# First expert visited: its turned rows by products with a one-hot matrix, its number changed to 1, and the shares behind its up product

## The reference, cut to what matters

```
h = rmsnorm(x) * g_ffn
g = argmax(h @ w_r1 + b_r1)                      # one of 4 groups, by token
e = top 2 of (h @ w_r2 + b_r2)[group g]          # two of its 4 experts
share = group probability * normalised expert probability
hid = silu(h @ w_gate[e]) * (h @ w_up[e])        # 1024 -> 256
out = x + sum over the two e of share * (hid @ w_down[e])   # 256 -> 1024
```

## Time and profile before

| | us |
|---|---|
| median of 3 runs | 1452.06 |
| the profiled execution, its own time | 1451.33 |
| its span in the trace | 1449.4 |
| last r_hot ready (DVE L2709) | 1221.9 |
| first transpose of expert rows (PE L1470) | 1234.9 |
| first up product starts (PE L1477) | 1237.8 |
| second up product starts | 1250.4 |
| last product of an expert ends (PE) | about 1431 |

### The profile page before, as it was taken

How to read it: one execution, slowest core, us unless ns; L and a number is a source line. 1 busy time by engine, 2 the same in 40 slices (tenths; PEclk the granted TensorE clock), 3 DMA queues, 4 the chain that set the end, 5 groups by cost and what they waited for, 6 DMA issues and landing times.

```text
span 1449.4 us, 16277 instructions
## 1 busy us (share of the span) xinstructions
PE 1326.3 (92%) x6144; PEld 982.7 (68%) x6144; DVE 563.8 (39%) x1294; ACT 539.9 (37%) x952; POOL 408.4 (28%) x203
## 2 busy tenths in 40 slices
PE   3999989889899999999998999999899996899996
PEld 3788666457678766765877777888787785444443
DVE  2164353534320135236897453234423315121225
ACT  4353434343542447445333554323433333111111
POOL 3255221014555222233423112543115322000002
PEclk9999999979999999999999999999999997899999
DMA  4232434013444221221322112432034605989915
GB/s 146 65 102 75 158 103 132 17 52 124 139 126 160 73 58 59 59 73 46 114 66 94 45 45 66 163 106 73 8 147 129 250 27 205 384 318 371 331 59 190
DMA packets 76474, 179.60 MB, mean 124 GB/s; under 512 B 11217, under 2 KB 22791, under 8 KB 69735
## 3 DMA queue, kind: packets, MB, share of 16 engines
q1 hardware_dynamic: 68656, 165.48, 33.7%
q0 software_dynamic: 2624, 8.41, 1.6%
q10 hardware_dynamic: 5110, 4.62, 1.1%
HBM read 153.32 MB, written 25.17 MB: 123 GB/s over the span
## 4 chain that ended last, share of the span: by engine, by line
PE 43%; DVE 8%; ACT 2%; issue 1%; DMA 1%; POOL 0%; DVEq 0%; ACTq 0%
PE ps L993 8%; PE ps L1477 8%; PE ps L995 8%; PE ps L994 8%; PE ps L1484 4%; DVE work L2551 1%; PE ps L1371 1%; PE ps L1354 1%; DVE dq L2560 1%; DVE best L2549 1%; PE ps L1470 1%; PE ps L1327 1%; DVE mix_lo L2330 1%; PE ps L1399 1%; PE ps L1361 1%
## 5 line engine op out<-in xcount | busy, mean ns | idle before, releaser
L877 POOL TENSOR_TENSOR w_lo<-raw,w_hi 128x1024 fp32r<-128x1024 f32 (+1 forms) x158 | 377.7, 2407 | 786.2 <-ACT w_hi L1691 786.2
L993 PE MATMUL ps<-w_hi,act_hi 128*128 128x512 f32 (+1 forms) x560 | 234.7, 419 | 6.9 <-POOL w_lo L877 3.6
L1691 ACT ACTIVATE w_hi<-raw 128x1024 fp32r<-128x1024 f32 (+1 forms) x158 | 158.9, 1033 | 169.3 <-PE ps L995 160.7
L994 PE MATMUL ps<-w_lo,act_hi 128*128 128x512 f32 (+1 forms) x560 | 220.3, 393 | 0.0
L995 PE MATMUL ps<-w_hi,act_lo 128*128 128x512 f32 (+1 forms) x560 | 219.6, 392 | 0.0
L993 PE MATMUL ps<-w_hi,mix_hi 128*128 128x512 f32 x320 | 131.8, 412 | 9.9 <-DVE mix_lo L2330 6.4
L993 PEld LDWEIGHTS ps<-w_hi,act_hi 128*128 128x128 f32 (+1 forms) x560 | 105.0, 187 | 47.2 <-issue 13.8
L995 PE MATMUL ps<-w_hi,mix_lo 128*128 128x512 f32 x320 | 126.3, 395 | 0.0
L994 PE MATMUL ps<-w_lo,mix_hi 128*128 128x512 f32 x320 | 126.2, 394 | 0.0
L995 PEld LDWEIGHTS ps<-w_hi,act_lo 128*128 128x128 f32 (+1 forms) x560 | 104.8, 187 | 25.4
L994 PEld LDWEIGHTS ps<-w_lo,act_hi 128*128 128x128 f32 (+1 forms) x560 | 105.0, 188 | 24.0 <-issue 1.5
(11 more groups left out here) (447 smaller groups left out, 1925.4 us busy)
## 6 DMA issues: line engine op xcount, KB each, us to landing
raw<-in_w_in SPq DMA_DIRECT2D x92, 512.0 KB, 3.5
gu<-in_w_gate SPq DMA_DIRECT2D x16, 1024.0 KB, 6.1
gu<-in_w_up SPq DMA_DIRECT2D x16, 1024.0 KB, 8.5
dn<-in_w_down SPq DMA_DIRECT2D x16, 1024.0 KB, 9.8
x_rows<-zeros SPq DMA_DIRECT2D x16, 512.0 KB, 4.9
raw<-in_w_out SPq DMA_DIRECT2D x16, 512.0 KB, 3.9
raw<-in_w_mem_kv SPq DMA_DIRECT2D x16, 512.0 KB, 3.7
xe<-x_rows SPq DMA_DIRECT2D x16, 512.0 KB, 9.1
```

Of the source, the lines that this page charges most:

```text
L877: pool.tensor_tensor(lo[:, 0:a], raw[:, g % RAW_SLOTS, 0:a], hi[:, 0:a].bitcast(F32), ALU.subtract).then_inc(*POOL.done(("w_lo", g)))
L993: pe.matmul(dst, l_hi, r_hi, start=start, stop=False, skip_group_check=skip)
L994: pe.matmul(dst, l_hi, r_lo, start=False, stop=False, skip_group_check=skip)
L1691: nc.scalar.activation(split_slot(g)[0][:, 0:a], raw[:, g % RAW_SLOTS, 0:a], ACTF.Copy).then_inc(*ACT.done(("w_hi", g)))
```

## The change

The expert visited first is now number 1, and number 0 the second (`expert_of`). Its rows aren't read back from DRAM. On VectorE `place` also makes a one-hot matrix for each token block, token by slot of expert 1. PE multiplies the normalised rows of each block with it (`x_hot(t)`), eight products per block, accumulated over the four blocks in banks 0 and 1; the sum is the turned rows, ready for the same two VectorE copies. The count of tokens becomes a step of its own (`counts`) behind `x_hot(3)`. The shares (`r_weights`), the overflow flag and both `last_hot` move behind the first up product, the making of `oh` (`last_oh`) being split from its use; the SiLU table is loaded at the end of ScalarE's `r_weights`. The up product waits for each half of `xeT` where it needs it. SP reads rows for visits 1, 2 and 3 at once, and issues set 5 (which lies over `xs_ffn`) behind the last `x_hot`.

```
+def expert_of(visit):
+    return (FIRST_E, 0)[visit] if visit < 2 else visit          # FIRST_E = 1

-    order += [("r_turn", 3), ("route", 1, 1), ("rank", 1), ("pos", 1), ("r_stat", 3), ("r_logits", 3), ("route", 2), ("rank", 2), ("pos", 2)]
-    order += [("r_weights",), ("last_hot", 0), ("over_flag",), ("x_turn", 0)]
+    order += [("r_turn", 3), ("x_hot", 0), ("route", 1, 1), ("rank", 1), ("pos", 1), ("r_stat", 3), ("r_logits", 3)]
+    order += [("x_hot", 1), ("x_hot", 2), ("route", 2), ("rank", 2), ("pos", 2), ("x_hot", 3), ("counts",), ("x_turn", 0)]
+    order += [("r_weights",)]
     for e in range(N_EXP):
         order += [("up", e)] + [("x_turn", e + 1)] * (e + 1 < N_EXP) + [("down", e - 1)] * (e > 0) + [("turn", e)]
-        if e == 2:
-            order += [("last_hot", 1)]
+        order += [("over_flag",)] * (e == 0) + [("last_hot", e - 1)] * (1 <= e <= 2) + [("last_oh", e)] * (e < 2)
...
             sp.wait_ge(scattered, 16 * 2 * NT)
-            for e in range(X_BUFS):
-                sp.dma_start(xe[:, e, :], expert_rows(x_rows, e)).then_inc(xe_in[e], 16)
+            for e in range(1, X_BUFS + 1):
+                sp.dma_start(xe[:, e % X_BUFS, :], expert_rows(x_rows, expert_of(e))).then_inc(xe_in[e % X_BUFS], 16)
             for e in (4, 5):
+                if e == 5:
+                    sp.wait_ge(*PE.after("xT", 0, 1))
                 load_up(sp, e, e, gu_in[e])
...
+            def x_hot(t):
+                if t == 0:
+                    for half in range(2):
+                        claim(half, (DVE, ("xeT", 0, half)))
+                pe.wait_ge(*ACT.after("xs_ffn", t))
+                pe.wait_ge(*DVE.after("hot", t))
+                for k in range(KC):
+                    mm = pe.matmul(ps[:, k // 4, P * (k % 4):P * (k % 4) + P], xs_ffn[:, t, P * k:P * k + P], oh[t // 2][:, t % 2, :],
+                                   start=(t == 0 and k % 4 == 0), stop=(t == NT - 1), skip_group_check=True)
+                    if t == NT - 1 and k % 4 == 3:
+                        mm.then_inc(*PE.done(("xT", 0, k // 4)))
...
             def up_product(bank, s, i, turned=None):
                 for k in range(KC):
+                    if turned is not None and k % 4 == 0:
+                        pe.wait_ge(*DVE.after("xeT", turned, k // 4))
                     mm = pe.matmul(ps[:, bank, :], xeT[:, i, k, :], gu[s][:, :, k, :], start=(k == 0), stop=(k == KC - 1))
...
                 act.wait_ge(*DVE.after("r_d"))
                 nc.scalar.activation(rt[:, 9, 0:4], rt[:, 9, 0:4], ACTF.Exp).then_inc(*ACT.done(("r_ed",)))
+                tables(SILU)
...
                 link(dve.tensor_tensor(r_at[:, a:b, :], r_hot[:, a:b, :], r_at[:, a:b, :], ALU.mult))
+                dve.wait_ge(*DVE.after("first_slots"))
+                for t in ts:
+                    dve.tensor_scalar(oh[t // 2][:, t % 2, :], first_slots[:, :], r_at[:, t, FIRST_E:FIRST_E + 1], None,
+                                      ALU.is_equal).then_inc(*DVE.done(("hot", t)))
...
-            def last_hot(i):
+            def last_oh(i):
...
                 hot.then_inc(*DVE.done(("oh", i)))
+
+            def last_hot(i):
+
                 dve.wait_ge(*PE.after("slot_share", i))
```

More of the change, by code:

```diff
@@ L158 @@
 E_SETS = 6
+FIRST_E = 1
 LAST_E = (N_EXP - 2, N_EXP - 1)
@@ L514, in program @@
         slots = sb("slots", [P, P], 129.75)
+        first_slots = sb("first_slots", [P, P], 130.25)
         tl = sb("tl", [P, 24], 133.75)
@@ L784, in first_sets @@
                         sp.wait_ge(*PE.after("m_O", NT * MEM_H - 1))
-                        load_up(sp, 0, 0, gu_in[0])
+                        load_up(sp, expert_of(0), 0, gu_in[0])
                     elif u == 1:
-                        load_down(sp, 0, 0, dn_in[0])
+                        load_down(sp, expert_of(0), 0, dn_in[0])
                 elif name == "w_out20":
@@ L790, in first_sets @@
                         sp.wait_ge(*PE.after("unit", first_unit["gate21"] + KC // 2 - 1))
-                        load_up(sp, 1, 1, gu_in[1])
+                        load_up(sp, expert_of(1), 1, gu_in[1])
                     elif u == 1:
-                        load_down(sp, 1, 1, dn_in[1])
+                        load_down(sp, expert_of(1), 1, dn_in[1])
                 elif name == "w_out21":
@@ L842, in _ @@
                     load_up(sp, e + E_SETS, e % E_SETS, gu_in[e % E_SETS])
-                if e + X_BUFS < N_EXP:
+                if 0 < e and e + X_BUFS < N_EXP:
                     sp.wait_ge(*PE.after("xT", e, 1))
@@ L854, in _ @@
                 sp.wait_ge(*DVE.after("ye", e - 1))
-                sp.dma_start(expert_rows(y_rows, e - 1), ye[:, (e - 1) % 2, :]).then_inc(ye_out[(e - 1) % 2], 16)
+                sp.dma_start(expert_rows(y_rows, expert_of(e - 1)), ye[:, (e - 1) % 2, :]).then_inc(ye_out[(e - 1) % 2], 16)
             for t in range(NT):
@@ L1456, in rank_rows, with counts @@
                 mm.then_inc(*PE.done(("ranked", i)))
[L1457 to L1462, removed]
+            def counts():
+                claim(6, (DVE, ("over",)))
+                for t in range(NT):
+                    mm = pe.matmul(ps[:, 6, 80:96], all_ones[:, :], r_hot[:, t, :], start=(t == 0), stop=(t == NT - 1),
+                                   skip_group_check=True)
+                mm.then_inc(*PE.done(("counts",)))
+            def x_hot(t):
[9 more added lines that the diff above has]
+                        mm.then_inc(*PE.done(("xT", 0, k // 4)))
             def x_turn(e):
+                if e == 0:
+                    return
                 for half in range(2):
                     claim(half, (DVE, ("xeT", e, half)))
-                pe.wait_ge(xe_in[e % X_BUFS], 16 * (e // X_BUFS + 1))
+                pe.wait_ge(xe_in[e % X_BUFS], 16 * ((e - 1) // X_BUFS + 1))
                 for k in range(KC):
@@ L1472, in x_turn, with up_product @@
                         tr.then_inc(*PE.done(("xT", e, k // 4)))
-            def up_product(bank, s, i):
+            def up_product(bank, s, i, turned=None):
                 for k in range(KC):
+                    if turned is not None and k % 4 == 0:
+                        pe.wait_ge(*DVE.after("xeT", turned, k // 4))
                     mm = pe.matmul(ps[:, bank, :], xeT[:, i, k, :], gu[s][:, :, k, :], start=(k == 0), stop=(k == KC - 1))
@@ L1497, in up @@
                 claim(2 + e % 2, (ACT, ("e_silu", e)), (DVE, ("hid", e)))
-                for half in range(2):
-                    pe.wait_ge(*DVE.after("xeT", e, half))
-                up_product(2 + e % 2, e % E_SETS, e % 2).then_inc(*PE.done(("up", e)))
+                up_product(2 + e % 2, e % E_SETS, e % 2, e).then_inc(*PE.done(("up", e)))
             def turn(e):
@@ L1658, in _ @@
                     rank_rows(*a)
+                elif step == "counts":
+                    counts()
+                elif step == "x_hot":
+                    x_hot(*a)
                 elif step == "x_turn":
@@ L2655, in r_start @@
                 dve.wait_ge(route_in, 16 * 8)
+                dve.tensor_scalar(first_slots[:, :], slots[:, :], float(FIRST_E), None, ALU.add).then_inc(*DVE.done(("first_slots",)))
                 dve.tensor_tensor(w_rg[:, :, :], w_r[:, :, :], gains[:, GAINS["g_ffn_2"]:GAINS["g_ffn_2"] + KC].unsqueeze(2).to_broadcast([P, KC, 20]),
@@ L3027, in _ @@
                      "mem_values": mem_values, "r_stat": r_stat, "r_logits": r_logits, "route": route, "pos": place, "r_weights": r_weights,
-                     "x_turn": x_turn, "up": up, "down": down, "last_hot": last_hot, "add": add, "last_rows": last_rows}
+                     "x_turn": x_turn, "up": up, "down": down, "last_oh": last_oh, "last_hot": last_hot, "add": add, "last_rows": last_rows}
             for step, *a in order:
```

## The result

| | before | changed |
|---|---|---|
| median, first set of runs | 1452.06 us (5) | 1439.07 us (5) |
| ratio, 95% interval | | 0.9898 [0.9872, 0.9924] |
| ratio of a second set (e1) | | 0.9893 [0.9874, 0.9913] |
| profiled execution, its own time / span | 1451.33 / 1449.4 us | 1434.36 / 1432.4 us |

The forecast was 1438.8 us, with 1435.3 to 1443.5 as the range. The two profiled executions differ by 17.0 us, more than the medians do. Part of that isn't the change's: the first `rank`, which stands ahead of nearly all of it, comes at 1197.02 here and came at 1199.38 before.

The account below looks back on a forecast made before the run. PE, busy 92% of the span, was taken as the bound, with time to gain in the seam before the experts and the second last_hot. Terms -12.3 - 1.3 + 0.3 = -13.3 us gave 1438.8 us, range 1435.3 to 1443.5.

Parts of the forecast that it names:

- part 1: Seam between routing and experts: one-hot products replace scatter wait, read and transposes; up(0) starts at 1228.2 against 1237.75.
- part 2: First up product: the clock comes back earlier within it, so it takes 8.0 us, before 9.05.
- part 3: From up(0)'s end to up(1): no table load (-1.28) and a half wait (-0.55) leave 1.8 to 1.9 of 3.6 us.
- part 4: Both last_hot on PE's path, oh made long before, no clock fall: -1.3 us (bounds -1.8 and +1.7).
- part 5: Expert visits: the second wait inside each up product costs 0.3 us in all (bounds 0 and 2.2); tail unchanged.
- Rival B: Expert visits: transfers catch up with PE, some 0.5 us wait each over six, giving 1441.8 us; chance 0.10.
- Rival A: Seam between routing and experts: the clock stays low throughout, giving 1445.3 us; chance 0.10.

Follow-up runs that it names:

- e1: The changed kernel run again with no edit: 1436.29 us median, ratio 0.9893 to the kernel before.
- e3: Changed kernel with all four blocks of one-hot products behind the last pos instead of in PE's gaps: 1445.25 us, ratio 0.9946 to the kernel before.
- e2: Changed kernel with the new order alone, no one-hot products, first visit's rows read back and transposed: 1447.57 us, ratio 0.9974 to the kernel before.
- e4: Changed kernel with the SiLU table loaded in front of the first SiLU again; one trace: up(1) 10.34 us behind up(0) instead of 9.06.
- e5: Changed kernel with both xeT halves awaited in front of the up product; one trace: up(1) 9.49 us behind up(0) instead of 9.06.
- e6: Changed kernel plus five idle products behind x_hot(2) and five behind the last rank; one trace: up(0) 28.0 us behind the first rank.
- e8: Changed kernel with counts before x_hot(3), last_hot(0) behind up(0), five idle products behind x_hot(2): 1438.81 us, ratio 0.9873 to the kernel before.
- e9: Changed kernel plus a 1 MB DRAM copy behind each refill of experts 6 to 13; one trace, 3.6 us longer than e1's from the rank.
- e12: Changed kernel with counts before x_hot(3) and last_hot(0) between up(0) and the second visit's transposes: 1435.49 us, ratio 0.9882 to the kernel before.
- e10: Changed kernel plus five idle products between the last rank and x_hot(3); one trace: up(0) 27.1 us behind the first rank.

## Why the prediction was right, by its steps

**The read and the scatter off the path, products in the gaps (part 1): right, and shown.** Up(0) starts 9.6 us sooner, 9.55 forecast. Step by step: `x_hot(0)` 1.8 us as taken from the attention's products; the last logits 1.8 us at full clock; VectorE's `rl`, late next as forecast, 17.95 us behind the first rank (17.97 forecast); `x_hot(1)` and (2) hidden with 1.6 us to spare (1.7 forecast); `x_hot(3)` 3.0 us from start to start (2.9); counts 1.3 (1.5). E3 shows the hiding: with it undone, 5.7 us come back.

**Up(0) (part 2): the mechanism right, the size off.** I took 8.0 us with part of it at half clock, and it took 7.1. The clock was back when up(0) began: 0.9 us more gained than forecast. Beside it the shares and the table load were hidden with 3.8 us to spare (4 forecast). Most of the difference between -13.3 and -14.6 is this term. In e2, where transposes and a wait for transfers stand in front, up(0) still takes 9.18. The Trainium skill's rule that transposes don't count as activity for the clock (page TensorE: Matmul & The Clock Gate, section Part 4: PE-mode transpose) agrees with that, but the wait in front of them would explain it too; no run separates the two. In e3 the clock came back (0.82 from 1207 to 1208) while PE was in the middle of eight transposes, behind some 2.6 us of products at half clock, so a rise can at least fall among transposes.

**Up(1) (part 3): right.** 1.7 us, of which e4 shows 1.28 for the table load and e5 0.43 for the half wait, where 0.55 had been taken.

**`last_hot` (part 4): right.** Two of them cost 1.7 us each (1246.33 to 1248.02), and the stall for `oh` and the fall of the clock behind it are gone: -1.4 for -1.3. E2, which has the new order without the products, shows the same 37.65 us from up(1) to up(4).

**Waits and transfers (part 5).** The waits inside the products cost nothing; the 0.3 us that I took was too much. **Rival B** went as far as its first step: the first write of `ye` lands after 18.3 us instead of 8.4 before, where 20 to 23 had been named (13 us x 0.425 is 5.5 MB more in the queue, not the 5 that I wrote). The refills now start against a fuller queue. The time to landing then falls to 15.2, 12.0 and 10.6 by the fourth visit, because the queue drains at 415 to 425 GB/s when there is work for it:

```profile
y_rows<-ye SPq DMA_DIRECT2D x1, 512.0 KB, 18.3
```

```profile
1262.00:1274.00 12.00, 12.00 (x37) 5.92 (x36) 2.41 (x4) 1.26 (x3) 0.00 (x0) 1.00 1.02 425
```

My mistake there was to read the 369 GB/s of the earlier trace rows as what the engines can do; it is what a visit asks for. By the Trainium skill's figure for HBM, some 358 GB/s for a core (page DMA: Bandwidth & Descriptors, section Where 436 GB/s comes from), the loop would have fallen behind; both rows are above it, and the measurement decides. **Rival A** appears in part: in e6, e8, e9 and e12 the clock fell at `x_hot(1)` and (2), which took 5.4 us instead of 3.8. In e9 and e12 the routing hides that, too: the last rank starts 22.2 us behind the first, as in e1.

## What to carry to other kernels

A round trip through DRAM that only permutes rows can be replaced by products with a one-hot matrix where TensorE is waiting anyway: four blocks of 1.8 us came for about 3 us on the path and removed two transfers and eight transposes. Put each block into the gap in front of a result that the slow engine is still making; the same products behind it cost 5.7 us more. And compare traces from a common instruction just ahead of the change to one behind it: from the first rank to up(4) the two profiles of the changed kernel agree to 0.1 us, where the whole moves by several. Last, a one-hot row made by comparison needs a number that no absent token can have: `r_at` is 0 for a token that didn't choose the expert, and 0 is also the first row of expert 0, so the expert visited first had to be number 1.

## What the runs showed that I had not expected

The start of the first rank lies between 1197.0 us (changed kernel) and 1203.3 (e6) in kernels whose code ahead of it is the same: 6.3 us of spread, over 40% of the effect measured. The kernel before lies within it, at 1199.38; its code ahead of the rank differs by one VectorE instruction (which makes `first_slots`) and by which of two experts' weights come first.

TensorE's clock fell to 0.50 in e6 while PE was at work without a pause in the trace. What it did before the fall was logits of 20 columns and ranks of 16, beside eight transposes and one block of 128 columns; in e1, with the same work, it didn't fall there. How the order of the work and the moment of the run share in this stays open.

The end of the program has two lengths. The last down product stands behind a wait of 2.28 us in every kernel, with the same code around it. In the profiles of e2, e4, e8, e9, e10 and e12 the clock fell to 0.50 behind that wait and the product took 5.3 to 5.4 us; in the other eight, the kernel before among them, it stayed at 1.00 and the product took 3.67. The changed kernel and e12:

```profile
1410.84 3.67 PE L1513 MATMUL ps<-dn,hidT 128*128 128x512 f32 x8 [2.28 <-DVE yl_lo L2845]
```

```profile
1411.08 5.33 PE L1513 MATMUL ps<-dn,hidT 128*128 128x512 f32 x8 [2.28 <-DVE yl_lo L2845]
```

That is 1.7 us on a product that no edit here touches, and about as much as e8, e10 and e12 had gained on the changed kernel ahead of it: all three end 235.4 to 235.6 us behind the first rank, against 235.3 to 235.4. Both profiles on which the -14.6 us rest have the short end. Why the clock falls behind the same wait in some executions and not in others stays open.
